# Softmax blocks turned two at a time by VectorE, in place of alternate blocks turned by TensorE

## What is computed

```python
scores = einsum('bnqhgd,bnkhd->bnhgqk', qb, kb) * (HEAD_DIM ** -0.5)
scores = where(mask, scores + bias, NEG_INF)
m = maximum(max(scores, axis=-1), sink)
p = exp(scores - m)
probs = p / (sum(p, axis=-1) + exp(sink - m))
out = einsum('bnhgqk,bnkhd->bnqhgd', probs, vb)
y_a = (out * silu(gate_a)) @ w_branch_a
```

## Time and profile before

| | |
|---|---|
| median of 3 runs | 901.44 us (901.38 to 901.56) |
| the profiled execution | 901.18 us |
| its span | 899.4 us |
| PE busy | 892.2 us, 99% |
| DVE, ACT, POOL busy | 632.3, 502.0, 523.5 us |

### The profile page before, as it was taken

One profiled execution on the slowest core, in us unless ns is written; L12 is line 12 of the kernel. 1 busy time (PEld: TensorE's weight loads), 2 busy tenths in 40 slices (PEclk: granted clock), 3 DMA queues, 4 the chain that ended last, 5 costly groups with the idle time before them and its releaser, 6 DMA issues.

```text
span 899.4 us, 12763 instructions
## 1 busy us (share of the span) xinstructions
PE 892.2 (99%) x4268; PEld 747.6 (83%) x4268; DVE 632.3 (70%) x1135; ACT 502.0 (56%) x982; POOL 523.5 (58%) x427
## 2 busy tenths in 40 slices
PE   9999999999999999999999999999999999999997
PEld 7888888888888888888888888888888888888886
DVE  6766795555555555546455589688789878989968
ACT  6554354776767676766766674344344434534562
POOL 4564335788888888887979667344442252042236
PEclk9999999999999999999999999999999999999999
DMA  9786664443434346534343453544188550435004
GB/s 316 189 198 150 223 208 106 153 108 104 135 103 131 106 126 159 174 107 132 103 136 93 121 156 106 188 150 122 43 321 300 188 210 1 141 128 200 1 1 187
DMA packets 170512, 130.90 MB, mean 146 GB/s; under 512 B 58552, under 2 KB 139472, under 8 KB 170320
## 3 DMA queue, kind: packets, MB, share of 16 engines
q1 hardware_dynamic: 168208, 126.66, 46.3%
q10 hardware_dynamic: 2240, 3.43, 1.1%
HBM read 93.87 MB, written 39.35 MB: 148 GB/s over the span
## 4 chain that ended last, share of the span: by engine, by line
PE 98%; DVE 1%; issue 0%; ACT 0%; DVEq 0%; POOLq 0%; POOL 0%; ACTq 0%
PE acc L1023 50%; PE acc L1205 11%; PE acc L876 10%; PE ps_m L1205 7%; PE ps_t L1205 7%; PE ps_t L1040 3%; PE ps_m L1071 3%; PE acc L966 2%; PE ps_t L1050 1%; PE ps_t L906 1%; PE ps_m L906 1%; PE ps_t L908 0%; PE acc L1097 0%; PE ps_m L908 0%; PE ps_t L892 0%
## 5 line engine op out<-in xcount | busy, mean ns | idle before, releaser
L1023 PE MATMUL acc<-mv,w_hi 128*128 128x512 f32 x1344 | 349.3, 391 | 0.0
L1023 PEld LDWEIGHTS acc<-mv,w_hi 128*128 128x128 f32 x1344 | 246.1, 188 | 46.5
L1023 PE MATMUL acc<-mv,w_lo 128*128 128x512 f32 x672 | 181.0, 391 | 0.0
L1820 POOL TENSOR_TENSOR w_lo<-sums,w_hi 128x1024 fp32r<-128x1024 f32 x48 | 117.7, 2454 | 62.2 <-ACT w_hi L1371 49.1
L1023 PEld LDWEIGHTS acc<-mv,w_lo 128*128 128x128 f32 x672 | 126.1, 188 | 28.0
L1820 POOL TENSOR_TENSOR w_lo<-raw,w_hi 128x1024 fp32r<-128x1024 f32 (+1 forms) x48 | 94.3, 1965 | 41.4 <-ACT w_hi L1364 34.3
L1575 ACT ACTIVATE prob<-neg_s,neg_max 128x129 f32<-128x129 f32 x128 | 50.7, 397 | 88.0 <-DVE neg_max L2152 87.9
L1205 PE MATMUL acc<-right,left 128*128 128x512 f32 x432 | 98.6, 389 | 0.0
L1205 PEld LDWEIGHTS acc<-right,left 128*128 128x128 f32 x432 | 81.0, 188 | 17.2 <-DVE left L2213 0.3
L876 PE MATMUL acc<-mv 128*128 128x512 f32 x288 | 69.4, 394 | 0.0
L1205 PE MATMUL ps_t<-right,left 128*128 128x512 f32 x288 | 67.2, 389 | 0.0
(11 more groups left out here) (286 smaller groups left out, 1702.1 us busy)
## 6 DMA issues: line engine op xcount, KB each, us to landing
raw<-in_w_in SPq DMA_DIRECT2D x56, 512.0 KB, 4.8
ht_d<-sums SPq DMA_DIRECT2D x8, 512.0 KB, 4.7
mix_d<-mix_b SPq DMA_DIRECT2D x8, 512.0 KB, 3.8
prob_d<-prob SPq DMA_DIRECT2D x32, 128.0 KB, 2.2
turned_in<-prob_d SPq DMA_DIRECT2D x128, 32.0 KB, 2.3
ga_d<-gate SPq DMA_DIRECT2D x16, 256.0 KB, 4.4
tb<-tb_d SPq DMA_DIRECT2D x4, 1024.0 KB, 5.3
ub<-mix_d SPq DMA_DIRECT2D x7, 512.0 KB, 3.5
```

Of the source, the lines that this page charges most:

```text
L1023: ins = nc.tensor.matmul(bank, (w_lo if y == 2 else w_hi)[:, left + k * P:left + (k + 1) * P], right[:, (OPW if y == 1 else 0) + k * HALF: ...
L1820: nc.gpsimd.tensor_tensor(w_lo[:, c], src, w_hi[:, c].bitcast(f32), ALU.subtract).then_inc(wlo_ok, 1)
```

## The change

All blocks are turned by DVE, at the block's scores step plus one. `transpose_p` and the two DVE instructions that split its result are gone. The two blocks of a couple j (blocks 2j and 2j+1) lie side by side in one buffer. SP stores them at step 3j+3 in four DMAs that put the 32x32 squares in their places in DRAM, in runs of 32 elements, and reads them back at step 3j+4 in one DMA. ACT's high half (step 3j+7), POOL's low half and mask (both at step 3j+8) are made for both blocks at once. PE multiplies both blocks by v at step 3j+9, the moving of the result is at 3j+10 and the gate at 3j+11, and `ga_d` is stored at steps 15 and 21. `ps_s` becomes two banks, so the scores of a block wait for the block before the last one instead of the last. The gate's first half has one buffer instead of two. The order in which attention's parts stand within a step, ahead of `after`, is as before.

The diff, cut to its core:

```diff
@@ -162,7 +163,7 @@
-    prob_d = nc.dram_tensor("prob_d", [4 * HEAD_PAIRS, P, 2 * P], f32)
+    prob_d = nc.dram_tensor("prob_d", [4 * HEAD_PAIRS, 4, P, P], f32)
@@ -213,16 +214,13 @@
-                prob = [sb(f"prob{b}", [P, 2 * SINK_W], f32, s1) for b in range(3)]
-                o_tmp = sb("o_tmp", [P, 256], f32, s1)
-                turned_in = sb("turned_in", [P, 256], f32, s1)
-                gate = [sb(f"gate{b}", [P, SEQ], f32, s1) for b in range(2)]
+                soft = sb("soft", [P, 2 * SOFT_W + 4 * SINK_W + 768], f32, s1)
+                gate = sb("gate", [P, 3 * HALF], f32, s1)
...
-                pt_pack = [sb(f"pt_pack{b}", [P, 512], f32r, s1) for b in range(2)]
-                pt_prev = [sb(f"pt_prev{b}", [P, 512], f32r, s1) for b in range(2)]
-                neg_s = sb("neg_s", [P, 4 * SINK_W], f32, s1)
+                pt_pack = sb("pt_pack", [P, 1024], f32r, s1)
+                pt_prev = sb("pt_prev", [P, 1024], f32r, s1)
@@ -253,7 +251,7 @@
-        ps_s, ps_p = ps_t[:, 0:512], ps_t[:, 512:768]
+        ps_s = (ps_t[:, 0:512], ps_t[:, 512:1024])
@@ -375,14 +374,33 @@
+        prob = (soft[:, 0:SOFT_W], soft[:, SOFT_W:2 * SOFT_W])
+        turned_in = soft[:, 2 * SOFT_W:2 * SOFT_W + 512]
+        o_tmp = soft[:, 2 * SOFT_W + 512:2 * SOFT_W + 768]
+        neg_s = soft[:, 2 * SOFT_W + 768:2 * SOFT_W + 768 + 4 * SINK_W]
+        v_part = (soft[:, 0:SEQ], soft[:, SEQ:2 * SEQ])
+        def gate_w(p, h):
+            return gate[:, 0:HALF] if h == 0 else gate[:, (p % 2 + 1) * HALF:(p % 2 + 2) * HALF]
...
-        def prob_w(s, h, width):
-            buf = prob[2] if s % 2 else prob[s // 2 % 2]
-            return buf[:, h * SINK_W:h * SINK_W + width]
+        def prob_at(s, h):
+            return 1 + ((1, 2) if s % 2 == 0 else (0, 3))[h] * P
+        def prob_w(s, h):
+            c = prob_at(s, h)
+            return prob[s // 2 % 2][:, c:c + P]
+        def exp_w(s, h):
+            c = prob_at(s, h) - (h == 0)
+            return prob[s // 2 % 2][:, c:c + SINK_W]
@@ -485,17 +503,9 @@
-        def even_at(k, lag):
-            return [2 * j for j in range(4) if 3 * j + lag == k]
-        def odd_at(k, lag):
-            return [2 * j + 1 for j in range(4) if 3 * j + lag == k]
-        def place(p, blk):
-            return 8 * p + (blk ^ 1) + 1
+        def couple_at(k, lag):
+            return [j for j in range(4) if 3 * j + lag == k]
@@ -651,31 +661,31 @@
-                sp.wait_ge(turn_ok, j + 1)
-                sp.dma_start(prob_d[j, :, :].rearrange("p (c j) -> p c j", c=2),
-                             prob[j % 2][:, :].rearrange("p (c j) -> p c j", c=2)[:, :, 0:P]).then_inc(prob_out, 16)
+                sp.wait_ge(turn_ok, 2 * j + 2)
+                for q in range(4):
+                    sp.dma_start(prob_d[j, :, :, :].rearrange("c (g a) (q b) -> q a c g b", g=4, q=4)[q],
+                                 prob[j % 2][32 * q:32 * (q + 1), 1:1 + 4 * P].rearrange("a (c g b) -> a c g b", c=4, g=4)
+                                 ).then_inc(prob_out[j % 2], 16)
...
-                sp.wait_ge(prob_out, 16 * (j + 1))
+                sp.wait_ge(prob_out[j % 2], 64 * (j // 2 + 1))
...
-                for g in range(4):
-                    sp.dma_start(turned_in[32 * g:32 * (g + 1), :].rearrange("a (c q b) -> a c q b", c=2, q=4),
-                                 prob_d[j, :, :].rearrange("(q a) (c g b) -> g a c q b", q=4, c=2, g=4)[g]).then_inc(prob_in, 16)
+                sp.dma_start(turned_in.rearrange("p (c x) -> p c x", c=4), prob_d[j, :, :, :].rearrange("c p x -> p c x")).then_inc(prob_in, 16)
...
-                for blk in even_at(k, 2):
-                    prob_away(4 * p + blk // 2)
-                for blk in even_at(k, 3):
-                    prob_back(4 * p + blk // 2)
+                for c in couple_at(k, 3):
+                    prob_away(4 * p + c)
+                for c in couple_at(k, 4):
+                    prob_back(4 * p + c)
...
-                if k in (13, 19):
-                    h = k // 19
+                if k in (15, 21):
+                    h = k // 21
...
-                                 gate[p % 2][:, h * HALF:(h + 1) * HALF]).then_inc(ga_out[h], 16)
+                                 gate_w(p, h)).then_inc(ga_out[h], 16)
@@ -1031,52 +1041,43 @@
                     pe.wait_ge(k_in, 64 * (1 if p == 0 else 2))
-                if s:
-                    pe.wait_ge(scores_used, s)
+                if s > 1:
+                    pe.wait_ge(scores_used, s - 1)
                 lo = P if blk == 0 else 0
...
                     for kbuf, a in ((k_hi, True), (k_lo, False)):
-                        ins = nc.tensor.matmul(ps_s[:, h * 256 + lo:(h + 1) * 256], q_st[h][:, blk * P:(blk + 1) * P],
+                        ins = nc.tensor.matmul(ps_s[s % 2][:, h * 256 + lo:(h + 1) * 256], q_st[h][:, blk * P:(blk + 1) * P],
                                                kbuf[:, kc + lo:kc + 256], start=a, stop=not a, skip_group_check=True)
...
-            def transpose_p(p, blk):
-                s = 8 * p + blk
-                pe.wait_ge(prob_ok, s + 1)
-                if s > 1:
-                    pe.wait_ge(ptl_ok, 4 * p + blk // 2)
-                for h in range(2):
-                    ins = nc.tensor.transpose(ps_p[:, h * P:(h + 1) * P], prob_w(s, h, P), ident[:, :])
-                ins.then_inc(pt_done, 1)
             def values(p, blk):
-                pe.wait_ge(pt_ok, place(p, blk))
-                if p == 0 and blk == 1:
+                pe.wait_ge(pt_ok, 4 * p + blk // 2 + 1)
+                if p == 0 and blk == 0:
                     pe.wait_ge(vlo_ok, 2)
-                if p == HEAD_PAIRS // 2 and blk == 1:
+                if p == HEAD_PAIRS // 2 and blk == 0:
                     pe.wait_ge(v_in, 16)
-                if p == HEAD_PAIRS // 2 and blk == 5:
+                if p == HEAD_PAIRS // 2 and blk == 4:
                     pe.wait_ge(v_out, 32)
                 g = 4 * p + blk // 2
-                if blk % 2 and g >= 2:
+                if blk % 2 == 0 and g >= 2:
                     pe.wait_ge(oadd_ok, g - 1)
...
                 kbs = (0,) if blk == 0 else (0, 1)
+                heads = slice(0, 4, 3) if blk % 2 else slice(1, 3)
                 for kb in kbs:
...
                     for y in range(2):
-                        ins = nc.tensor.matmul(o, v_st[:, v0:v0 + P], pt[blk % 2][:, y * 256:(y + 1) * 256].rearrange("p (h c) -> p h c", h=2),
+                        ins = nc.tensor.matmul(o, v_st[:, v0:v0 + P], pt[:, y * 512:(y + 1) * 512].rearrange("p (x c) -> p x c", x=4)[:, heads, :],
                                                start=(kb == 0 and y == 0), stop=(kb == kbs[-1] and y == 1), skip_group_check=True)
...
             def attend(p, k):
-                for blk in odd_at(k, 6) + even_at(k, 7):
-                    values(p, blk)
-                for blk in odd_at(k, 3):
-                    transpose_p(p, blk)
+                for c in couple_at(k, 9):
+                    values(p, 2 * c)
+                    values(p, 2 * c + 1)
                 for blk in blocks_at(k, 0):
@@ -1176,8 +1177,7 @@
-                    pe.wait_ge(ptl_ok, 4 * HEAD_PAIRS)
-                    pe.wait_ge(pt_ok, 8 * HEAD_PAIRS)
+                    pe.wait_ge(scores_used, 8 * HEAD_PAIRS)
@@ -1567,30 +1567,27 @@
                     act.wait_ge(sink_ok, p + 1)
-                if s % 2 and s > 1:
-                    act.wait_ge(pt_done, s // 2)
                 if s % 2 == 0 and s >= 4:
-                    act.wait_ge(prob_out, 16 * (s // 2 - 1))
+                    act.wait_ge(prob_out[s // 2 % 2], 64 * (s // 4))
                 for h in range(2):
-                    ins = nc.scalar.activation(prob_w(s, h, SINK_W), neg_w(blk, h), ACT.Exp, scale=-1.0, bias=neg_max[:, head(blk, h)],
+                    ins = nc.scalar.activation(exp_w(s, h), neg_w(blk, h), ACT.Exp, scale=-1.0, bias=neg_max[:, head(blk, h)],
                                                accum_out=row_sum[:, head(blk, h)])
...
                 for h in range(2):
-                    w = prob_w(8 * p + blk, h, P)
+                    w = prob_w(8 * p + blk, h)
                     ins = nc.scalar.activation(w, w, ACT.Copy, scale=inv_den[:, head(blk, h)])
...
-            def turned_hi(p, blk):
-                j = 4 * p + blk // 2
-                act.wait_ge(prob_in, 64 * (j + 1))
+            def turned_hi(j):
+                act.wait_ge(prob_in, 16 * (j + 1))
                 if j:
...
                     act.wait_ge(v_out, 16)
-                nc.scalar.activation(pt_pack[0][:, 0:256], turned_in[:, :], ACT.Copy).then_inc(turn_hi, 1)
+                nc.scalar.activation(pt_pack[:, 0:512], turned_in, ACT.Copy).then_inc(turn_hi, 1)
@@ -1599,10 +1596,9 @@
-                for blk in even_at(k, 5):
-                    turned_hi(p, blk)
-                if k in (8, 11, 14, 17):
-                    g = (k - 8) // 3
```

(70 more changed lines are left out.)

24 lines of the change are left out of this document (13 added, 11 removed).

## The result

| | before | after |
|---|---|---|
| median | 901.41 us (901.34 to 901.56) | 926.58 us (923.55 to 929.97) |
| the profiled execution | 901.18 us | 923.55 us |
| its span | 899.4 us | 921.8 us |
| its mean granted clock | 1.000 | 0.993 |

The ratio is 1.028, with a 95% interval from 1.0232 to 1.0328: the changed kernel is slower by 25 us. The forecast was 903.5, with a range from 896.5 to 909. The direction came true and the size did not. The two profiled executions differ by 22.4 us, and the traces are compared on that. The four executions of the changed kernel took 923.6, 923.7, 929.4 and 930.0 us, and only the first was traced, so what the two long ones lost beyond it (their mean granted clock is 0.988 and 0.990) is not shown.

The account below looks back on a forecast made before the run. PE was taken as the bound, busy 99% of the span, with POOL having the least room. Transposes and an old wait gave -7.5 us, waits for POOL's mask +9.5, so +2.0: 903.5 us predicted, range 896.5 to 909.

Parts of the forecast that it names:

- What PE gives back: On PE: 32 pairs of transposes at 0.22 us, 7.0 us off; with the removed score wait, 7.5 off.
- The old wait of the last head pair: PE's one attention wait, costing 0.54 us, removed by the second score bank; 0.5 us counted as gained.
- Where the steps come to lie: PE's shifted schedule, third head pair: step 9 starts at 282.95, and step 12 wants values of couple 1 at 292.83.
- POOL's chain: POOL, steps 8 to 12: couple 1's mask done at 294.03; PE waits 1.2 us, costing 1.36 in seven head pairs, 9.5.
- ACT's high half: ACT at step 7: turned_hi of couple 0 starts at 279.58, done at 280.20; mask ready 282.8, in time by a hair.
- DVE has room: DVE: trades the odd blocks' two splits for two transposes; busy 27.6 of 50 us, so no cost counted.
- Other places, at nothing: Steps after 12, couples 2 and 3, DVE, the gate's single buffer and SP's queue: no time added.
- four issues take 2.54 us, so about 3.2 per couple before and after: SP's queue: four stores and one load replace one store and four loads, with issue time per couple unchanged.
- Rival 2: 128-byte stores land slowly, SP holds the second raw load, POOL's sums start late; 910.5 us at 7 us landing; chance 0.06.
- a raw load that SP issues late behind slow stores: The sign in SP's queue that would show the slow-store rival true and the forecast wrong.
- Rival 3: ACT's eviction at step 10 late behind turned_hi and result moving; 0.15 us wait, no addition; 1 us beyond gives 910.5; chance 0.16.
- The sum: Whole kernel: -7.5 + 9.5 = +2.0 us on the profiled 901.18, giving 903.2, or 903.4 on the median.

Follow-up runs that it names:

- e11: e9 with DVE turning each block at its old place, one step after its scores; 899.10 us, ratio 0.9973.
- e6: e5 with DVE turning each block one step later, behind the scores of the next block; 905.42 us, ratio 1.0043.
- e5: Changed kernel with the skew DMA's 128 rows as outermost dimension in place of its two heads, same bytes; 909.56 us, ratio 1.009.
- e9: e8 with prob_back two steps later and e6's later turning by DVE; 904.95 us, ratio 1.0046.
- e1: Changed kernel with one store per couple in 2 KB runs and four loads in 128-byte runs; 915.61 us, ratio 1.0154.
- e3: Changed kernel with DVE instead of POOL making the sums of the even column pairs; 928.61 us, ratio 1.0297.
- e4: Changed kernel with the edits of e1 and e3 together; 916.50 us, ratio 1.0161.
- e2: Changed kernel with SP issuing a step's raw loads ahead of its attention DMAs; 910.60 us, ratio 1.0097.
- e8: e5 and e2 together, with everything from turned_hi on, and SP's second reload of v, one step later; 903.14 us, ratio 1.0016.

## Why the prediction was right or wrong

**What PE gives back: right.** The 7.0 us of transposes are there: e11's head pair is 0.95 shorter for 0.88 forecast. The old wait of the last head pair is gone too, but POOL's and ACT's take its place.

**Where the steps come to lie, and POOL's chain: the mechanism right, the sizes near.** The subtraction takes 1.28 (1.29 forecast), the mask 1.09 (1.15), there is no idle time but 0.35, and PE waits at step 12 for the mask. Where nothing else is late (e6) the wait is 0.86 for 1.2, and with a restart of 0.22 for 0.16 it costs 1.08 a head pair instead of 1.36.

**ACT's high half, and "DVE has room": wrong, a small step.** I argued from DVE's share, 27.6 of 50 us, and not from its order. DVE stands 0.76 us at the turning of block 3, waiting for ACT's division, with the scores of block 4 behind it; the exps, ACT's copy, and POOL's chain are late by that. I had couple 0 in time by a hair at step 9, and it is 0.53 late. Undone by e6, it is worth 4.1 us: 47.67 - 46.88 = 0.8 in each of the five head pairs that have both waits in e5, and the one wait for ACT's `c` in the last head pair takes a part back (0.93 in e5, 1.45 in e6).

**Other places, at nothing, SP: the step that failed.** I wrote "four issues take 2.54 us, so about 3.2 per couple before and after", and covered the stores' landing with POOL's work at couples 2 and 3. For couple 0, the first to be stored, I gave no landing at all, and did not ask what the moved stores now follow in the DMA engines. The skew DMA keeps about two of the 16 busy for some 10 us (267.89 to about 278); the stores issued a step later land late beside it, `prob_back` waits for the last of them, the raw loads and the stores of couple 1 are then issued in a bunch behind that, and ACT (17.0 us, 5.3 before) and POOL (9.3, 2.4 before) wait for the raw loads. That was 17.0 us of the 25 (e5), of which PE's longer waits are one part and the three drops of the clock (4.4 us in the profiled execution) another. The four issues took 3.25 and 4.42 us there, not 2.54.

**Rival 2: its consequence came, by another cause and in another place.** "SP holds the second raw load" is what happened, and its sign, "a raw load that SP issues late behind slow stores", was there to see. But I had it from the size of the pieces. The Trainium skill ("DMA: Bandwidth & Descriptors", Specifications) says that pieces below 512 bytes are read, modified and written. The trace doesn't show that it costs here: with 128-byte pieces (64 KB in a store) and the skew DMA spread, the median landing of a store is 2.9 us (e5) and 2.2 (e9), beside 2.2 for pieces of 512 bytes (128 KB), and with 2 KB pieces (256 KB) and the narrow skew DMA it was 4.5 (e1). And I had it at couples 2 and 3, where the raw load of step 13 stands, not at couple 0.

**Rival 3: right behind, with help.** e3 and e4 took the weight off POOL and PE then waited for ACT's `c`. But both gave the sums to DVE, for which ACT then waited longer (70.8 and 58.1 us against 34.9), so they don't show that the order worked out in rival 3 is enough. It was priced as no addition to POOL's wait, and in the seven head pairs of e5 and e6, where DVE has no sums, PE doesn't wait for `c` at all.

**The sum.** -7.5 + 9.5 = +2.0 was forecast. With e6's figures the same sum is -7.5 + 7 x 1.08 = +0.1, and e6 measures +4.0: the rest is in single waits that I did not count (1.45 behind ACT's `c` at 527.89, 0.87 at the reload of the keys, 0.76 in the last head pair). To this come 4.1 for DVE's order and 17.0 for SP's: 905.4 + 4.1 + 17.0 = 926.6, which closes by itself, since the two terms are the differences between these runs. Whether all of the 17.0 goes through the raw loads was tested by e2 alone, which keeps the slow landing and still takes off 16.0 us.

## What to carry to other kernels

When a change moves a DMA, look at what is already in flight on every queue at its new place, and at what stands behind the instruction that waits for its landing; the duration from a row of before holds only for the traffic it was taken in. For an in-order engine, read what is queued behind each new wait, whatever share of its time is free. And where several engines are late by nearly the same amount, relieve the source they share: work taken from the one that PE waits for shows the next one, and can hold that one up from its new place.

## What the runs showed of the hardware that was not expected

**A DMA whose outermost dimension has size two ran on about two of the 16 engines.** The outermost dimension of the skew DMA is its two heads. The share was 0.14 and 0.15 after the other traffic had ended, at some 50 GB/s, and it took about 10 us; with the 128 rows outermost the same bytes landed in 4.5 us. The Trainium skill says the same ("DMA: Bandwidth & Descriptors", Rules for kernel authors): the number of engines follows from the slowest dimension that isn't of size one, and an outermost dimension smaller than 16 keeps the DMA on at most that many. The trace agrees.

**Such a DMA holds up the landing of stores from another engine's queue.** It is issued by ACT and the stores by SP; with it on two engines the longest landing was 10.0 us, spread out it was 5.1. It doesn't hold up every store: of the four of couple 0 in the third head pair the first landed in 2.3 us and the last in 8.5. The Trainium skill has a reason ("DMA: Bandwidth & Descriptors", Queues, rings and completion order): the write to the semaphore lands only after every earlier write of that DMA engine, across its queues. By that a store is reported late even if its own data has gone. The runs show the lateness and not which of the two it is, the data or the report.

**A wait of PE can cost its length again.** After the waits of 2.41 to 2.80 us the granted clock was at 0.50 in a stretch of 2 us and at 0.78 to 0.99 in the next, 1.4 to 1.5 us lost each time, about half the wait; after the one of 3.24 us in e8 it was at 0.50 for about 6 us, some 3 us lost.
